# Value slots of a fused two-block transformer kernel: each product of 512 columns written as two of 256

## The chip, the cores and the metric

The kernel runs on one core of one Trainium2 chip. The metric is the device time of the core in microseconds, less being better. Before the change the median of three runs is 1130.42 us (1130.38 to 1130.47).

## What is computed

The input is one sequence of 256 tokens of width 1024 in float32. Two hybrid layers (an mLSTM branch, a gated linear attention branch and a sparse attention branch side by side) are followed by a block of feed-forward, mixer and feed-forward. Almost all of the arithmetic is a product with a large weight matrix. For this change the products matter whose result is wanted with tokens on the partitions, that is the "value" columns:

```python
p = split_columns(rmsnorm(x, norm_g) @ w_in)      # ml_v, gla_v, dsa_v, dsa_q, dsa_k among its columns
...
z = n @ w_in[l]
v = z[..., 2 * A_WIDTH:3 * A_WIDTH]
zg = jax.nn.gelu(z[..., 3 * A_WIDTH:])
```

## The kernel before, in words

All weights are one long list of 364 "slots". A slot is 128 partitions by 1024 float32, and one transfer of 512 KB (line 301) brings it to `raw`. ScalarE (line 480) rounds it into part 0 of `ring`, the high part in the format fp32r. GpSimd (line 366, twice 512 columns) or, for some slots, VectorE (line 1000) writes the difference as part 1, the low part. `raw` and `ring` hold five slots each. The activations `xs` are kept as a high and a low part too. A product with a weight slot is three TensorE passes (`PARTS`): weight high by x high, weight low by x high, weight high by x low.

TensorE takes the slots in order. Each slot begins with a wait for its low part (`arrived`, `here`) and its last product signals `slots_used`, which lets ScalarE round a later slot into its place. Three forms of slot exist:

- `tile_product` (line 1713): the weight tile is stationary, `xs` of 256 tokens is the moving operand; 24 products of 256 columns for a slot.
- `sum_slot` (line 1798): the same with `ys` moving; 24 products of 256 columns.
- `value_slot` (line 1776): here a tile of 128 tokens of `xs` is stationary and 512 columns of the weights in `ring` are moving; for each of two token tiles, two k tiles and three passes there is one product of 512 columns, 12 for a slot. Four such slots in a row complete two PSUM banks, one for each token tile. With `by_tile` the 512 columns lie in four runs of 128.

There are 56 value slots: in each of the two hybrid layers the slots 6 to 13, 18 to 25 and 42 to 49 (table `VALUE_SLOTS`), and in the mixer the slots 8 to 15. Between slots TensorE does small work of the attention branches, "jobs" (tables `jobs` and `jobs2`), for instance `level` (line 1958), `index_logits` (1907, 1909), `ml_scores` (2032, 2035), `scores2` (2201, 2202). Of the 56 value slots 20 follow another slot directly (6, 7, 10, 12, 18, 42, 43, 44 of each layer, and 8, 10, 11, 12 of the mixer), and 36 follow a job. Each of the 672 products has a weight load (LDWEIGHTS) of its own.

Of the kernel before, what the change touches and what calls it, by code (L numbers as in the profile page):

```python
# [28 lines left out]
P = 128  # L29
D = 1024  # L30
T = 256
# [123 lines left out]
def build(nc, d, out):  # L155
    ctx = ExitStack()
    with ctx:
        def sb(name, shape, dt=F32):
            return ctx.enter_context(nc.sbuf_tensor(name, shape, dt))
# [15 lines left out]
        xs = sb("xs", [P, KT, 2, T], F32R)  # L175
# [53 lines left out]
        def branch(k, part):  # L229

            return ys[:, k, part, :] if k < 4 else xs[:, k - 4, part, :]
# [18 lines left out]
        ps = [ctx.enter_context(nc.psum_tensor(f"ps{b}", [P, 512], F32)) for b in range(8)]  # L250
# [1439 lines left out]
        def _(pe):  # L1690
            mm = pe.matmul
# [13 lines left out]
            def tile_product(bank, half, slot, rhs, ks=range(KT), at=0, ready=None, freed=False, first=True, final=True):  # L1705

                order = [(k, w, x) for k in ks for w, x in PARTS]
                if ready:
                    order = [(k, w, 0) for k in ks for w in (0, 1)] + [(k, 0, 1) for k in ks]
                for i, (k, wp, xp) in enumerate(order):  # L1710
                    if ready and wp == 0:
                        ready(k, xp)
                    last = mm(ps[bank][:, half * T:(half + 1) * T],  # L1713
                              ring[:, slot % RING, wp, (at + k) * P:(at + k + 1) * P], rhs(k, xp),
                              start=(first and i == 0), stop=(final and i == len(order) - 1))
                    if freed and (wp, xp) == PARTS[-1] and k < KT - 1:
                        last.then_inc(S["xs_free"], 1)
                return last
# [49 lines left out]
            def value_slot(banks, slot, q, by_tile=False):  # L1768

                for tt in range(2):  # L1770
                    for k in range(2):
                        for j, (wp, xp) in enumerate(PARTS):
                            w = ring[:, slot % RING, wp, k * 512:(k + 1) * 512].rearrange("p (j c) -> p j c", j=4)
                            if by_tile:
                                w = ring[:, slot % RING, wp, :].rearrange("p (j k c) -> p k j c", j=4, k=2)[:, k]
                            last = mm(ps[banks[tt]][:, :].rearrange("p (j c) -> p j c", j=4),  # L1776
                                      xs[:, 2 * q + k, xp, tt * P:(tt + 1) * P], w,
                                      start=(q == 0 and k == 0 and j == 0), stop=(q == 3 and k == 1 and j == 2))
                last.then_inc(S["slots_used"], 1)

            def sum_slot_lo_last(slot, at, y_lo):
# [60 lines left out]
            for it in range(LAYERS):  # L1842
# [238 lines left out]
                for p in range(IN_SLOTS):  # L2081
                    done = results_at(p)
                    if p in VALUE_SLOTS:
                        r, q = VALUE_SLOTS[p]
# [7 lines left out]
                        if r == EARLY:  # L2092
                            pe.wait_ge(S["x_hi"], it * KT + 2 * q + 2)
                            pe.wait_ge(S["x_lo"], it * KT + 2 * q + 2)
                        value_slot((r % 4, (r + 1) % 4), p, q, r < R_GQ)
                    else:
                        r = done[0]
# [158 lines left out]
            for p in range(MIX_IN_SLOTS + GATE_SLOTS):  # L2256
                slot = MIX_AT + p
                if 8 <= p < 16:
                    r, q = 8 + (p - 8) // 4 * 2, p % 4
                    if q == 0:  # L2260
                        m_bank_free(r)
                        m_bank_free(r + 1)
                    here(slot)
                    if r == M_EARLY:
                        pe.wait_ge(S["x_hi"], LAYERS * KT + 2 * q + 2)
                        pe.wait_ge(S["x_lo"], LAYERS * KT + 2 * q + 2)
                    value_slot((r % 4, r % 4 + 1), slot, q)
                else:
                    r = m_results_at(p)[0]
                    if r == 2:  # L2270
                        here(slot)
                        around_squares(2, slot, 3)
                    elif r > 1:
                        m_bank_free(r)
                        here(slot)
                        tile_product(r % 4, 0, slot, xs_part,
                                     freed=(r == M_EARLY - 1 or r == 31)).then_inc(S["slots_used"], 1)
                    if r == 1:
                        here(MIX_AT)
                        here(MIX_AT + 1)  # L2280
                        first_two((0, MIX_AT), (1, MIX_AT + 1), xs_part, early_ready(3))
                for job, *which in jobs2.get(p, ()):
                    job(*which)
            for n in range(KT):
# [7 lines left out]
                for g in range(2):  # L2292
                    last = tile_product(n % 4, g, slot, lambda k, part: branch(4 * g + k, part), range(4), at=4 * g,
                                        ready=(lambda k, part: pe.wait_ge(
                                            S["b_lo" if part else "b_hi"], 4 * g + k + 1)) if n == 0 else None)
# [28 lines left out]
            for b in (5, 6):  # L2324
                for c in range(2):
                    last = mm(ps[b][:, c * P:(c + 1) * P], rms[:, 512 + c:513 + c].broadcast_to((P, P)), ident,
                              start=True, stop=True)
# [129 lines left out]
```

## Time and profile before

| | |
|---|---|
| median of three runs | 1130.42 us |
| the profiled execution's own time | 1130.05 us |
| its span, first to last instruction | 1128.3 us |
| TensorE (PE) busy | 1118.7 us, 8976 products |
| TensorE weight loads (PEld) busy | 1065.4 us, 8976 loads |
| VectorE, ScalarE, GpSimd busy | 711.0, 663.6, 732.1 us |
| granted TensorE clock | 0.998 |

Products overlap in the records: one of 256 columns is recorded as 276 ns long though the next starts 113 ns later. So the time that a product costs is read from stretches of equal products in the chain of waits (its time divided by its count), not from the recorded length of one.

### The profile page before, as it was taken

What the parts mean: (1) busy time and instruction counts of PE and PEld (TensorE: products, weight loads), DVE (VectorE), ACT (ScalarE), POOL (GpSimd) and SP (SyncE); (2) the same over time, 40 slices, a digit from 0 to 9 for tenths busy, and PEclk for the clock granted to TensorE, in tenths of its full rate; (3) what the DMA queues carried; (4) which work ended last, traced back from release to release, by engine and by line L of the source; (5) the groups of instructions that cost most, each with busy time, mean ns of one, the idle gap of its engine ahead of it and who ended that gap; (6) DMA issues with size and microseconds to landing.
All of it is one profiled execution on the core that took longest, in us unless ns stands there. A gap on an engine that the chain in (4) does not pass through costs nothing.

```text
span 1128.3 us, 22357 instructions
## 1 busy us (share of the span) xinstructions
PE 1118.7 (99%) x8976; PEld 1065.4 (94%) x8976; DVE 711.0 (63%) x1262; ACT 663.6 (59%) x1096; POOL 732.1 (65%) x577
## 2 busy tenths in 40 slices
PE   8999999999999999999999999999999999999997
PEld 7888998999988799899999999999899999999997
DVE  6886644566588775264857655556768667655554
ACT  7676854476577577446646544446566547544444
POOL 6787697667488868865765654445865774544442
PEclk9999999999999999999999999999999999999999
DMA  8553354546555534545566755664644654665650
GB/s 319 185 180 130 121 181 151 171 160 211 169 169 169 167 123 150 187 135 186 169 206 202 234 189 190 197 200 144 221 146 138 200 187 163 225 196 190 188 186 38
DMA packets 63895, 199.49 MB, mean 177 GB/s; under 512 B 6992, under 2 KB 17968, under 8 KB 63792
## 3 DMA queue, kind: packets, MB, share of 16 engines
q1 hardware_dynamic: 61920, 194.99, 52.9%
q10 hardware_dynamic: 1872, 3.08, 0.8%
q8 instruction: 71, 1.16, 0.4%
q14 instruction: 32, 0.26, 0.1%
HBM read 196.21 MB, written 1.84 MB: 176 GB/s over the span
## 4 chain that ended last, share of the span: by engine, by line
PE 97%; ACT 1%; DMA 1%; DVE 0%; issue 0%; POOLq 0%; SPq 0%; ACTq 0%
PE ps L1713 51%; PE ps L1798 19%; PE ps L1776 14%; PE ps L1958 2%; PE ps L1749 1%; PE ps L2052 1%; PE ps L2135 1%; PE ps L2032 1%; PE ps L2062 1%; DMA x<-in_x 1%; PE ps L1732 1%; PE ps L1993 1%; PE ps L2053 0%; PE ps L1932 0%; PE ps L2019 0%; PE ps L2035 0%
## 5 line engine op out<-in xcount | busy, mean ns | idle before, releaser
L366 POOL TENSOR_TENSOR ring<-raw,ring 128x512 fp32r<-128x512 f32 x516 | 699.6, 1362 | 370.6 <-ACT ring L480 349.4
L1713 PE MATMUL ps<-xs,ring 128*128 128x256 f32 x5040 | 598.5, 278 | 1.0 <-DVE mq L1038 0.9
L1713 PEld LDWEIGHTS ps<-xs,ring 128*128 128x128 f32 x5040 | 582.9, 188 | 5.9 <-issue 3.2
L480 ACT ACTIVATE ring<-raw 128x1024 fp32r<-128x1024 f32 x364 | 383.2, 1057 | 215.4 <-PE ps L1713 119.2
L1798 PE MATMUL ps<-ys,ring 128*128 128x256 f32 x1920 | 224.4, 276 | 0.0
L1798 PEld LDWEIGHTS ps<-ys,ring 128*128 128x128 f32 x1920 | 220.7, 188 | 0.0
L1000 DVE TENSOR_TENSOR ring<-raw,ring 128x1024 fp32r<-128x1024 f32 x106 | 141.7, 1337 | 68.4 <-ACT ring L480 67.8
L1776 PE MATMUL ps<-ring,xs 128*128 128x512 f32 x672 | 165.0, 398 | 0.0
L1776 PEld LDWEIGHTS ps<-ring,xs 128*128 128x128 f32 x672 | 123.6, 188 | 26.8 <-issue 1.3
L1313 DVE SCALAR_TENSOR_TENSOR ca<-ps,par,ca 128x253 f32<-128x253 f32 (+2 forms) x96 | 45.9, 478 | 34.4 <-ACT ca L564 33.0
L1457 DVE SCALAR_TENSOR_TENSOR ca<-ps,rms 128x256 f32<-128x256 f32 x44 | 18.6, 422 | 48.6 <-PE ps L1713 48.6
L1452 DVE SCALAR_TENSOR_TENSOR ex<-ps,rms 128x256 f32<-128x256 f32 x44 | 18.6, 423 | 45.1 <-PE ps L1713 44.9
L1062 DVE TENSOR_TENSOR ys<-y,ys 128x256 fp32r<-128x256 f32 x32 | 31.7, 991 | 19.5 <-ACT ys L721 19.5
L809 ACT ACTIVATE ys<-ca 128x256 fp32r<-128x256 f32 x44 | 18.4, 418 | 34.8 <-DVE ca L1466 34.8
L1062 DVE TENSOR_TENSOR ys<-ca,ys 128x256 fp32r<-128x256 f32 x44 | 30.4, 691 | 11.0 <-ACT ys L809 11.0
L581 ACT ACTIVATE ex<-ps 128x256 f32<-128x256 f32 x32 | 12.2, 382 | 35.0 <-PE ps L1713 34.9
L1462 DVE TENSOR_TENSOR ca<-ca,ex 128x256 f32<-128x256 f32 x44 | 30.8, 700 | 1.5
L564 ACT ACTIVATE ca<-ps,par 128x256 f32<-128x256 f32 x32 | 17.9, 560 | 21.0 <-PE ps L1713 21.0
L497 ACT ACTIVATE xs<-x,par 128x256 fp32r<-128x256 f32 x40 | 16.7, 496 | 12.8 <-DVE x L1072 9.6
L1369 DVE SCALAR_TENSOR_TENSOR ps<-ex,ps 128x256 f32<-128x256 f32 x32 | 13.6, 424 | 15.2 <-ACT ex L581 15.2
L1466 DVE SCALAR_TENSOR_TENSOR ca<-ex,ca 128x256 f32<-128x256 f32 x44 | 22.2, 505 | 1.4
L1749 PE MATMUL ps<-xs,ring 128*128 128x256 f32 x192 | 22.4, 276 | 0.0
(288 smaller groups left out, 1033.0 us busy)
## 6 DMA issues: line engine op xcount, KB each, us to landing
raw<-in_w SPq DMA_DIRECT2D x364, 512.0 KB, 3.5
y<-bias_rows SPq DMA_DIRECT2D x6, 256.0 KB, 4.6
out_y<-y SPq DMA_DIRECT2D x4, 256.0 KB, 2.3
const<-in_const SPq DMA_DIRECT2D x1, 896.0 KB, 12.3
bias_rows<-lg ACTq DMA_DIRECT2D x1, 768.0 KB, 7.1
x<-in_x ACTq DMA_DIRECT2D x1, 512.0 KB, 4.4
x<-in_x SPq DMA_DIRECT2D x1, 512.0 KB, 6.7
dec<-in_wT ACTq DMA_DIRECT2D x1, 512.0 KB, 3.6
```

The lines of the kernel that those rows point to most:

```text
L366: last = pool.tensor_tensor(ring[:, g % RING, 1, part], raw[:, g % RAW, part], ring[:, g % RING, 0, part].bitcast(F32), ALU.subtract)
L480: act.activation(ring[:, g % RING, 0, :], raw[:, g % RAW, :], ACT.Copy).then_inc(S["hi"], 1)
L1000: tt(ring[:, g % RING, 1, :], raw[:, g % RAW, :], ring[:, g % RING, 0, :].bitcast(F32), ALU.subtract).then_inc(lo[g % RAW], 1)
L1062: tt(ys[:, at, 1, :], src, ys[:, at, 0, :].bitcast(F32), ALU.subtract).then_inc(S["y_lo"], 1)
L1313: ins = stt(dst[:, late:T], bank[:, 0:T - late], w[:, j:j + 1], dst[:, late:T], ALU.mult, ALU.add)
L1462: step(tt(ca[:, f % 2, :], ca[:, f % 2, :], ex[:, 2 + f % 2, :], ALU.mult))
L1466: stt(ca[:, f % 2, :], ex[:, f % 2, :], 1.0, ca[:, f % 2, :], ALU.add, ALU.mult)\
L1713: last = mm(ps[bank][:, half * T:(half + 1) * T], ring[:, slot % RING, wp, (at + k) * P:(at + k + 1) * P], rhs(k, xp), start=(first and i ...
L1749: return mm(ps[bank][:, 0:T], ring[:, slot % RING, wp, k * P:(k + 1) * P], rhs(k, xp), start=start, stop=stop)
L1776: last = mm(ps[banks[tt]][:, :].rearrange("p (j c) -> p j c", j=4), xs[:, 2 * q + k, xp, tt * P:(tt + 1) * P], w, start=(q == 0 and k == 0 ...
L1798: ins = mm(ps[4 + n // 2][:, n % 2 * T:(n % 2 + 1) * T], ring[:, slot % RING, wp, n * P:(n + 1) * P], ys[:, at, xp, :], start=(first and n ...
L1958: last = mm(second(ps[6 + e][:, (2 * tt + pr) * P:(2 * tt + pr + 1) * P]), kk[rows, keys], second(qq[rows, queries]), start=True, stop=True)
```

## The change

In `value_slot` each product of 512 columns becomes two of 256, one for each half of the bank, with the same stationary tile of `xs`. The bank is started by the first of them alone; the second half relies on the cleared state of the bank. Nothing else is changed: the order of slots and jobs, the waits and the signals stay.

```diff
-                            last = mm(ps[banks[tt]][:, :].rearrange("p (j c) -> p j c", j=4),
-                                      xs[:, 2 * q + k, xp, tt * P:(tt + 1) * P], w,
-                                      start=(q == 0 and k == 0 and j == 0), stop=(q == 3 and k == 1 and j == 2))
+                            for hf in range(2):
+                                last = mm(ps[banks[tt]][:, hf * T:(hf + 1) * T].rearrange("p (j c) -> p j c", j=2),
+                                          xs[:, 2 * q + k, xp, tt * P:(tt + 1) * P], w[:, 2 * hf:2 * hf + 2],
+                                          start=(q == 0 and k == 0 and j == 0 and hf == 0),
+                                          stop=(q == 3 and k == 1 and j == 2), skip_group_check=True)
                 last.then_inc(S["slots_used"], 1)
```

## Rows read from the trace of the kernel before

**Rows 1.** The page: busy time of the engines, and the granted clock.

```profile
PE 1118.7 (99%) x8976; PEld 1065.4 (94%) x8976; DVE 711.0 (63%) x1262; ACT 663.6 (59%) x1096; POOL 732.1 (65%) x577
...
PEclk9999999999999999999999999999999999999999
```

**Rows 2.** The page: the chain that ended last, shares by line.

```profile
PE ps L1713 51%; PE ps L1798 19%; PE ps L1776 14%; PE ps L1958 2%; PE ps L1749 1%; PE ps L2052 1%; PE ps L2135 1%; PE ps L2032 1%; PE ps L2062 1%; DMA x<-in_x 1%; PE ps L1732 1%; PE ps L1993 1%; PE ps L2053 0%; PE ps L1932 0%; PE ps L2019 0%; PE ps L2035 0%
```

**Rows 3.** Groups of instructions: busy us, mean ns of one, idle before, releaser.

```profile
L1713 PE MATMUL ps<-xs,ring 128*128 128x256 f32 x5040 | 598.5, 278 | 1.0 <-DVE mq L1038 0.9
L1713 PEld LDWEIGHTS ps<-xs,ring 128*128 128x128 f32 x5040 | 582.9, 188 | 5.9 <-issue 3.2
...
L1776 PE MATMUL ps<-ring,xs 128*128 128x512 f32 x672 | 165.0, 398 | 0.0
L1776 PEld LDWEIGHTS ps<-ring,xs 128*128 128x128 f32 x672 | 123.6, 188 | 26.8 <-issue 1.3
```

**Rows 4.** The waits: who waited for whom, us in total, times, longest.

```profile
POOL ring L366 <- ACT ring L480: 349.4, 145, 9.5
ACT ring L480 <- PE ps L1713: 119.2, 81, 2.0
...
ACT ring L480 <- PE ps L1776: 22.7, 12, 3.0
```

**Rows 5.** The chain in order of time (start, us, what): slots that follow slots.

```profile
138.85 19.05 PE ps L1713 x168
157.91 8.24 PE ps L1776 x36
...
203.92 29.94 PE ps L1713 x264
...
261.84 43.52 PE ps L1798 x384
```

**Rows 6.** The chain, 185 to 194.5 us: slots of both forms around a job.

```profile
185.00 2.75 PE ps L1776 x12
187.75 0.86 PE ps L2032 x4
188.61 0.45 PE ps L2035 x4
189.06 5.47 PE ps L1713 x48
```

**Rows 7.** The chain, 66 to 111 us: slots before and after line 1958.

```profile
81.70 2.96 PE ps L1776 x12
84.66 1.04 PE ps L1958 x16
...
107.40 2.94 PE ps L1713 x24
```

**Rows 8.** The chain in the mixer, 805 to 835 us.

```profile
805.97 11.01 PE ps L1776 x48
...
817.52 0.43 PE ps L2202 x2
817.96 2.75 PE ps L1776 x12
...
828.51 2.74 PE ps L1713 x24
...
831.80 0.43 PE ps L2202 x2
832.23 2.83 PE ps L1713 x24
```

**Rows 9.** The chain: slots 4 to 7 of the first layer, 6 and 7 of the second.

```profile
23.42 5.92 PE ps L1713 x48
29.34 5.60 PE ps L1776 x24
...
322.56 5.49 PE ps L1776 x24
```

## Prediction

> **What bounds the kernel now.** I began with the busy times and the clock [rows 1]. TensorE is busy for 1118.7 of 1128.3 us, and its clock is granted in full in every slice, so it runs at the upper of its two levels, 2.4 GHz, throughout. The shares of the chain say the same [rows 2]: lines 1713, 1798 and 1776, all products with weights, are 84% of it, and the value slots (1776) are 14% or about 158 us. The groups [rows 3] show no idle time ahead of the 672 products of line 1776. The suppliers are not late either: GpSimd, which finishes a slot, stands 349.4 us waiting for ScalarE, and ScalarE stands 119.2 us waiting for line 1713 and 22.7 us for line 1776 to free a place [rows 4]. So the end is set by how fast TensorE takes products one behind the other, and each nanosecond saved or lost on one of them reaches the end, unless the supply becomes late; it would have to be late by a few tens of nanoseconds for each slot, where it now waits for TensorE.
>
> **The prices.** The question is then whether two products of 256 columns take longer than one of 512. The chain in order of time answers it for this kernel. Where slots follow slots [rows 5], 36 products of 512 columns take 8.24 us, 228.9 ns each. The 168 products of 256 columns ahead of them take 19.05 us, 113.4 ns each; 264 later ones take 29.94 us (113.4 ns) and 384 of line 1798 43.52 us (113.3 ns). A slot is thus 2.747 us in the old form and 24 x 113.4 = 2.722 us in the new one: the change would gain 0.025 us for such a slot.
>
> Behind a job [rows 6] the old form takes 2.75 us for a slot, and two slots of line 1713 behind a similar job 5.47 us, 2.735 us each: 0.015 us better. Around line 1958 [rows 7] a value slot takes 2.96 us, a slot of line 1713 entered from the same line 2.94 us. I take 0.01 us for all slots behind jobs, since both numbers are rounded to it and other slots of line 1713 show 2.74 us [rows 8].
>
> There is an exception. Some slots of line 1713 run at a slower pace throughout, not only at their start: behind line 2202 a slot takes 2.83 us [rows 8], 118 ns a product, while the value slot that stands behind the same line takes 2.75 us, 229 ns a product of 512. Three more slots of that pair of lines later on repeat it. The slow pace is also carried from slot to slot: in the first layer the value slots 6 and 7 take 5.60 us, 233.3 ns a product, behind 48 products of line 1713 that take 5.92 us, while the same two slots in the second layer take 5.49 us, 228.8 ns [rows 9]. So a product has two paces here, 113.4 or 118 ns for 256 columns and 229 or 233 ns for 512. In the slow pace two halves cost 236 ns against 233, and, worse, a place that is quick for 512 columns may be slow for 256, as behind line 2202: 2.83 - 2.75 = 0.08 us lost for a slot.
>
> **The change part by part.**
> - Removed: 672 products of 512 columns with their loads. Added: 1344 of 256 with 1344 loads. Loads take 188 ns each [rows 3], longer than the pace of 113 ns, but line 1713 has a load for each product too, and keeps the pace; so I cost the added loads at nothing. That cover is gone only if a load could no longer start early; the whole 188 ns would then be seen.
> - Value slots that follow slots, without the mixer's 10 to 12 and the first layer's 6 and 7: 15 x 0.025 = 0.38 us gained.
> - Value slots behind jobs, without the mixer's 9, 13 and 15, which stand behind line 2202: 33 x 0.01 = 0.33 us gained.
> - The mixer's slots 9, 13 and 15, and 10 to 12 that follow 9 directly and would inherit its pace: 6 x 0.08 = 0.48 us lost.
> - The first layer's 6 and 7: 2 x 2.83 against 5.60 us, 0.06 us lost.
> - Nothing is moved past a wait or a queue, and the last product of a slot ends where it did: signals, evacuations and transfers follow within tens of nanoseconds. The start flag stands on one product in place of one; nothing waits on it.
>
> The sum is -0.38 - 0.33 + 0.48 + 0.06 = -0.17 us. On the profiled execution's 1130.05 us (span 1128.3) this is 1129.9 us; the median of the runs is 0.37 us above it, so I give 1130.42 - 0.17, rounded to 1130.2 us. No row shows a 256-column product with `ring` moving and `xs` stationary, so the pace is bounded from both sides: below by 113.3 ns in every slot, 672 x (228.9 - 226.6) = 1.5 us gained; above by 118 ns in every slot, 56 x 0.08 = 4.5 us lost. I take the quick pace except where a slot of line 1713 shows the slow one, because nearly all of its rows are quick.
>
> A rule speaks against the change. If 512 columns took 228.9 ns because of a cost for each product, two products would pay it twice. The rows say that there is none: doubling the 256 columns of line 1713 gives 226.8 ns, less than 228.9. By the Trainium skill (TensorE: Matmul & The Clock Gate, "Back-to-back issue gap") products at the full clock start N / 2.4 + 2.5 ns apart, and so one more product costs 2.5 ns: an estimate of 672 x 2.5 = 1.7 us lost. The trace disagrees with both figures of that rule, 113.4 ns where it gives 109.2 and 228.9 where it gives 215.8.
>
> **The rivals.** A measurement of this kernel can tell about 0.2%, 2.3 us, from no change; I judge them by that.
>
> 1. *Quick pace everywhere.* The slow pace comes from something at line 2202 that fits line 1713 only. Then 20 x 0.025 + 36 x 0.01 to 0.015 gives 0.9 to 1.0 us, up to 1.5 us by the pace alone: 1128.9 to 1129.5 us. For it: most rows are quick. Against: value slots do fall into the slow pace [rows 9].
> 2. *A surcharge for each product with these operands.* The 2.1 ns by which 512 columns exceed twice 113.4 may belong to the moving operand in `ring` and be paid once a product. Then a pair takes 226.8 + 2 x 2.1 = 231.0 ns, and 672 x 2.1 = 1.4 us are lost: 1131.8 us. For it: the surplus is seen only where `ring` is moving. Against: it could as well grow with the columns. The skill's rule named above points the same way.
> 3. *The slow pace everywhere (slower).* The place is the entry into a value slot behind a job; the slow pace, once entered, lasts to the next job, as in [rows 9]. Each slot loses 0.08 us, all 56 lose 4.5 us: 1134.9 us. It decides from 35 slow slots on (35 x 0.08 less 21 x 0.025 is 2.3 us). For it: line 2202 does just this. Against: behind lines 2035 and 1958 line 1713 is quick [rows 6, 7], and these jobs stand ahead of most value slots.
> 4. *Halves quicker than any row of that form.* Four products behind one another at line 2035 take 0.45 us, 112.5 ns each [rows 6]. At that pace a pair takes 225 ns and 672 x 3.9 = 2.6 us are gained: 1127.8 us. Nothing but that small job speaks for it.
> 5. *The loads are seen.* If the second load of the same tile of `xs` couldn't start under the first half, 672 x up to 188 ns = 126 us would be lost, 1256.7 us. Against: the first two passes of a k tile share their tile already, and the group is not slower for it than 228.9 ns.
>
> That the change doesn't do what it says (the two products or their loads being merged again) is ruled out by the counts: the first two passes share a stationary tile now, and there are still 672 loads for 672 products [rows 3]. If it were so, nothing would change.
>
> **How the numbers follow.** The forecast (a mixture of paces, 1129.6 to 1131.0) has a chance of 0.45, the quick pace everywhere 0.25, the surcharge 0.14, the slow pace everywhere or nearly so 0.09, quicker halves 0.05, seen loads 0.02. The first three are all within 0.2%: 0.84. Faster by more has 0.05, slower by more 0.11. The range is to hold the first three cases, the lower bound of rival 1 and the estimate by the rule included: 1128.6 to 1132.3 us.
>
> **What the profile of the changed kernel would show.** There should be 9648 products and as many loads, with 1344 of 256 columns in the value line; in the chain, stretches of 24 of them at 2.72 to 2.75 us where 12 stood at 2.75 us, and 2.83 us in the mixer behind line 2202 (now a few lines lower). The waits of ScalarE and GpSimd should be unchanged to a few us, the clock full. The prediction is wrong if the value slots' share of the chain changes by over 2.3 us, if idle time shows ahead of them, or if time changes outside of them.

## Result: slower by 0.25%, and the profile after

The changed kernel takes 1133.21 us (median of nine runs, 1132.11 to 1133.72) against 1130.42 us; the ratio is 1.0025 with a 95% interval of 1.0016 to 1.0033. That is 2.8 us slower, outside the range of 1128.6 to 1132.3 us and against a chance of 0.11 for slower by more than 0.2%. The profiled execution of the changed kernel has a span of 1131.0 us, 2.7 us longer than before, so its trace holds about the loss of the medians. (The own times of the two profiled executions lie 3.4 us apart, 1133.46 and 1130.05 us; 0.7 us of that lies outside the spans.)

The page of the kernel after, busy times and clock; they answer to [rows 1]:

```profile
PE 1121.3 (99%) x9648; PEld 1098.9 (97%) x9648; DVE 710.5 (63%) x1262; ACT 663.6 (59%) x1096; POOL 731.5 (65%) x577
...
PEclk9999999999999999999999999999999999999999
```

The groups of the same page, which answer to [rows 3]:

```profile
L1713 PE MATMUL ps<-xs,ring 128*128 128x256 f32 x5040 | 598.8, 278 | 1.2 <-DVE mq L1038 1.1
...
L1777 PE MATMUL ps<-ring,xs 128*128 128x256 f32 x1344 | 167.4, 281 | 0.0
L1777 PEld LDWEIGHTS ps<-ring,xs 128*128 128x128 f32 x1344 | 160.3, 188 | 2.3 <-issue 1.3
```

The counts are as forecast, the clock is full, line 1713 is what it was (598.8 us against 598.5), and no idle time stands ahead of the value line. Its busy time went from 165.0 to 167.4 us. So the loss is in the pace of the half-products, and the chain in order of time (start, us, what) shows where. First, value slots that follow slots and enter behind line 1713, against [rows 5]:

```profile
139.68 19.05 PE ps L1713 x168
158.73 8.16 PE ps L1777 x72
```

Three slots in 8.16 us, 113.3 ns a half-product; they took 8.24 us. This is the small gain that the forecast counted. Next, value slots behind jobs, and a pair of slots of line 1713, against [rows 6]:

```profile
181.26 2.83 PE ps L1777 x24
...
186.05 2.83 PE ps L1777 x24
...
190.19 5.47 PE ps L1713 x48
```

The first and the last of these stretches stand right behind the same job, `ml_scores`. Line 1713 still takes 2.735 us a slot there, but the value slots now take 2.83 us where they took 2.75, 118 ns a half-product. The level job and the mixer, against [rows 7, 8]:

```profile
73.68 3.02 PE ps L1777 x24
```

```profile
808.06 11.31 PE ps L1777 x96
...
820.36 2.82 PE ps L1777 x24
...
823.83 2.83 PE ps L1777 x24
```

Of the 56 value slots 42 end at a pace of 118 ns a half-product and 14 at 113.4 ns. The difference of each slot can be summed from the starts of the products in the two traces. Of the 42, most lose 0.06 to 0.08 us (three, slots 6 and 7 of the first layer and 13 of the second, which were in the slow pace before too, lose 0.03 us), together 2.87 us. The 14 gain 0.02 to 0.04 us each, together 0.38 us. That is 2.5 us net of the 2.7 us between the spans; of the rest, line 1713 is 0.35 us longer in the same count and smaller lines make up the remainder in both directions. Twelve of the 14 quick slots follow a slot or a stream of line 1713 directly; the other two (8 of the first layer, 9 of the second) stand behind a job and come back to the quick pace. All such counts are of one traced execution each.

### The profile page after: what moved, and what is told of

Its sections match the earlier page's. It is cut to its first block, busy times and chain, and to the rows that moved or that the text cites. A ratio compares the mean times of both kernels' runs of the same rounds, so it can differ in the third digit from the quotient of the medians.

```text
span 1131.0 us, 23701 instructions
## 1 busy us (share of the span) xinstructions
PE 1121.3 (99%) x9648; PEld 1098.9 (97%) x9648; DVE 710.5 (63%) x1262; ACT 663.6 (59%) x1096; POOL 731.5 (65%) x577
## 4 chain that ended last, share of the span: by engine, by line
PE 96%; DMA 1%; ACT 1%; DVE 1%; SPq 0%; issue 0%; POOLq 0%; ACTq 0%
PE ps L1713 51%; PE ps L1800 19%; PE ps L1777 14%; PE ps L1960 2%; PE ps L1749 1%; DMA par<-in_par 1%; PE ps L2054 1%; PE ps L2137 1%; PE ps L2034 1%; PE ps L2064 1%; PE ps L1995 1%; PE ps L2055 0%; PE ps L1934 0%; PE ps L2021 0%; PE ps L2037 0%; PE ps L2204 0%
## 5 line engine op out<-in xcount | busy, mean ns | idle before, releaser
L1713 PE MATMUL ps<-xs,ring 128*128 128x256 f32 x5040 | 598.8, 278 | 1.2 <-DVE mq L1038 1.1
L1777 PE MATMUL ps<-ring,xs 128*128 128x256 f32 x1344 | 167.4, 281 | 0.0
L1777 PEld LDWEIGHTS ps<-ring,xs 128*128 128x128 f32 x1344 | 160.3, 188 | 2.3 <-issue 1.3
```

The costliest lines, as they stand in the source:

```text
L1713: last = mm(ps[bank][:, half * T:(half + 1) * T], ring[:, slot % RING, wp, (at + k) * P:(at + k + 1) * P], rhs(k, xp), start=(first and i ...
L1777: last = mm(ps[banks[tt]][:, hf * T:(hf + 1) * T].rearrange("p (j c) -> p j c", j=2), xs[:, 2 * q + k, xp, tt * P:(tt + 1) * P], w[:, 2 * ...
```

## The experiments

They ran beside the kernel before on the same chip; its median is given each time. Theories are named by the letters of the expectations: A is that the slow pace is picked up at the entry behind a job and kept, B that any half-product costs more.

**Which slots lose.** `value_slot` gets a flag that is true for slots which follow another slot directly.

The diff is against the kernel before, in part:

```diff
-                            last = mm(ps[banks[tt]][:, :].rearrange("p (j c) -> p j c", j=4),
...
+                            step = 2 if follows else 4
+                            for c in range(0, 4, step):
+                                last = mm(ps[banks[tt]][:, c * P:(c + step) * P].rearrange("p (j c) -> p j c", j=step),
...
```

> Only the 20 value slots that follow another slot directly are split; the 36 behind jobs keep products of 512 columns. Theory A (the pace of 118 ns is picked up at the entry behind a job and kept by half-products): slots that follow a quick slot run at 2.72 us, so the kernel gains up to 20 x 0.025 = 0.5 us over the kernel before, 1129.9 to 1130.4 us, unless the mixer's slots 10 to 12 (behind slot 9, itself behind a job) are slow, which costs 3 x 0.08 us. Theory B (a surcharge of halves of this kind wherever they stand): 672 x 20/56 = 240 products cost 20/56 of the loss, +1.0 us, 1131.4 us.

Measured: 1130.27 us against 1130.28 (ratio 1.0001, 0.9992 to 1.001). The complement (`not follows`):

> Only the 36 value slots behind jobs are split. Theory A: nearly all of the loss is here, 33 to 36 slots at 2.83 us (3.02 around the level job) in place of 2.75 (2.96), +2.5 to +3.0 us against the kernel before, 1132.9 to 1133.4 us. Theory B: 36/56 of the loss, +1.8 us, 1132.2 us.

Measured: 1132.61 us against 1130.28 (1.0021, 1.0012 to 1.003). The loss is mainly in the slots behind jobs, as A says: by their traces the value slots of e1 take 0.3 us more than before and those of e2 2.1 us. By the medians alone B's 1.0 and 1.8 us aren't excluded; what speaks against B are the quick stretches, 8.16 us for three split slots in the changed kernel. But in e1 the chain of the mixer holds something that A did not foresee:

```profile
805.67 11.22 PE ps L1778 x84
```

These are one whole slot of 12 products and three split ones of 24. A whole slot took 2.75 us at this place before (11.01 us for four, [rows 8]); that leaves 8.47 us for the split ones behind it, 118 ns a half-product, though the slot ahead of them was at the quick 229 ns. So halves can be slow behind a whole slot that was quick.

**A whole first product.** The narrow form of A was tried the other way round: the first product of each slot stays whole. The rest of the edit is that of e1.

```diff
...
+                            step = 2 if tt or k or j else 4
...
```

> All slots are split, except that the first product of each slot keeps its 512 columns. If the pace is set by how the second product's load falls behind the first product at the entry (theory A in its narrow form: behind a job the gap from first to second start is about 203 ns with 256 columns and 314 ns with 512), a whole first product lets the later ones start quickly: slots at 2.72 to 2.75 us, -0.5 to -1 us, about 1129.7 us. If the slow pace is a property of halves of this kind (theories B and C), 11/12 of the loss stays, +2.5 us, 1132.9 us.

Measured: 1134.26 us against 1130.28 (1.0036, 1.0024 to 1.0049), worse than with all products split, and against the narrow form. Even the three slots behind the quick stream of line 1713 are slow now:

```profile
158.50 8.48 PE ps L1778 x69
```

They took 8.16 us with all products split and 8.24 us with none. Less the three whole products at 229 ns this is 118 ns for each of the 66 halves. Of the 56 slots 50 are slow now, against 42. It isn't a strict rule: slots 13, 20 and 24 of both layers, all behind jobs, run their halves at 113.4 ns though each begins with a whole product.

**The order of the products.** The half was made the outer loop (e3, which keeps `PARTS`), then the passes were also reordered so that no tile of x is loaded twice in a row (e5, whose diff against the changed kernel this is, in part):

```diff
                 for tt in range(2):
-                    for k in range(2):
-                        for j, (wp, xp) in enumerate(PARTS):
...
-                            for hf in range(2):
+                    for hf in range(2):
+                        for k in range(2):
+                            for j, (wp, xp) in enumerate(((0, 0), (0, 1), (1, 0))):
...
```

> All 56 slots are split, but for each token tile the six products of the left half come first, then the six of the right half, so the PSUM half changes once and the stationary tile is not loaded twice for each pass. Theory A as it stands (entry alone, the order of products does not matter): 118 ns in some 42 slots as in the changed kernel, +2.8 us, 1133.2 us. Theory C (the slow pace is held by the repeated load of the same tile and the alternation between halves, which line 1713 does not have): the pace falls back to 113.4 ns as in line 1713, 56 slots gain, -0.9 to -1.5 us, 1129 to 1129.5 us.

> All slots split, left half outermost, and the three passes in the order high by high, weight high by x low, weight low by x high, so that no two products in a row load the same tile of x; the moving tile is what repeats, as in line 1713. Theory D (the slow pace is kept because a stationary tile is loaded twice in a row, which line 1713 never does): slots behind jobs fall back to 113.4 ns within a few products, 56 quick slots, -0.9 to -1.5 us against the kernel before, about 1129.2 us. Theory E (the pace once picked up is kept by any slot with x stationary and the ring moving, whatever the order): 118 ns in some 42 slots again, +2.6 us, 1132.9 us.

Measured: 1132.93 us against 1130.28 (1.0026, 1.0017 to 1.0035) and 1133.00 us against 1130.44 (1.0024, 1.0014 to 1.0033). Behind the same `ml_scores` a slot of e5 still takes 2.83 us:

```profile
167.42 2.83 PE ps L1777 x24
```

In both kernels 39 slots are slow. Only slots of the first layer differ from the changed kernel: 6, 7, 9 and 10 are quick here and 8 is slow. Theories C and D are refuted: neither the change of PSUM halves after each product nor a repeated load is the cause. The same order of passes in `tile_product` (line 1713) and in whole value products:

> The kernel before, value slots whole, but line 1713 takes its passes as high by high, weight high by x low, weight low by x high, so that each weight tile is loaded twice in a row. Theory D: line 1713 slots behind jobs, about 50 of them, keep the pace of 118 ns (2.83 us in place of 2.74), up to +4 us, and slots that follow one another carry it, perhaps more. Theory E: no change beyond 0.5 us, 1130.3 us.

> The kernel before, whole products of 512 columns, with the order of passes high by high, weight high by x low, weight low by x high. In the kernel before the start-to-start time is 226 ns behind the first pass, whose tile the next product loads again, and 229 to 231 ns behind the other two. Theory D extended to whole products: with no tile repeated the 226 ns goes or moves, up to 672/3 x 4 ns = +0.9 us. Theory E: the pace of 228.9 ns stays, within 0.3 us of the kernel before, 1130.3 us.

Measured: 1130.42 us against 1130.44 (1.0, 0.9991 to 1.0009) and 1130.55 us against 1130.44 (1.0001, 0.9992 to 1.0009). Nothing moves, which agrees.

**The loads.** Three of four value slots use stationary tiles of 64 tokens; the results of the other 64 are left out.

```diff
+                            n = 64 if q else P
                             for hf in range(2):
-                                last = mm(ps[banks[tt]][:, hf * T:(hf + 1) * T].rearrange("p (j c) -> p j c", j=2),
-                                          xs[:, 2 * q + k, xp, tt * P:(tt + 1) * P], w[:, 2 * hf:2 * hf + 2],
+                                last = mm(ps[banks[tt]][0:n, hf * T:(hf + 1) * T].rearrange("p (j c) -> p j c", j=2),
+                                          xs[:, 2 * q + k, xp, tt * P:tt * P + n], w[:, 2 * hf:2 * hf + 2],
```

> The changed kernel, with stationary tiles of 64 tokens in place of 128 in three of four value slots (all but the first slot of each group of four): the results of the other 64 tokens of each tile are left out there. The 42 slots so changed have loads of half the columns. Theory F (the pace of halves is set by the weight load, which barely fits under 256 columns): those slots run at or below 113.3 ns even behind jobs, -1 us or more against the kernel before. Theory G (the columns of the product set it, the load only its start): 118 ns stays behind jobs, +2.7 us, as in the changed kernel.

Measured: 1132.15 us against 1130.44 (1.0016, 1.0007 to 1.0025). One line of the trace gives the loads (min, median, max ns), and the chain the slots behind a job:

```profile
L1778 PEld LDWEIGHTS ps<-ring,xs x1344: 132/134/192, 28.7 to 828.4; 128*64 128x64 f32 x144, 128*128 128x128 f32 x48
```

```profile
77.66 2.80 PE ps L1778 x24
...
86.06 2.83 PE ps L1778 x24
```

The first slot has loads of 64 columns (134 ns in place of 188), the other is a first slot of its group with loads of 128. Halving the load takes 0.03 us from a slot (116.7 in place of 118 ns a half-product), but it doesn't come back to 113.4 ns. So the pace is not that of a load that barely fits, though the load has a part in it.

**Whose operands.** Only the operands of the 1344 half-products were changed, so these kernels compute something else than the reference and serve for their time alone. The diff is that of e11, which exchanges both; e9 has its stationary tile alone, e10 its moving operand alone.

```diff
-                                          xs[:, 2 * q + k, xp, tt * P:(tt + 1) * P], w[:, 2 * hf:2 * hf + 2],
+                                          ring[:, slot % RING, wp, (2 * k + tt) * P:(2 * k + tt + 1) * P], xs[:, 2 * q + k, xp, :].rearrange("p (j c) -> p j c", j=2),
```

> The changed kernel with the stationary tile taken from the ring (the same slot) in place of xs, the moving operand unchanged; the values computed are not the reference's, only the number and shape of products and loads are kept. Theory H (loads from xs keep the slow pace): behind jobs the pace falls to 113.4 ns within some products as in line 1713, -0.9 to -1.5 us against the kernel before. Theory I (a moving operand in the ring keeps it): 118 ns in some 42 slots, +2.7 us.

> The changed kernel with the moving operand taken from xs (256 tokens) in place of the ring, the stationary tile from xs as now; the values are again not the reference's. Theory H: 118 ns stays in some 42 slots, +2.7 us against the kernel before. Theory I: quick behind most jobs, -0.9 to -1.5 us. If both this and e9 are slow, it is neither operand alone but their place in the program; if both are quick, it is the pair.

> A control: in the value slots, 24 products with the stationary tile from the ring and the moving operand from xs, the operands of line 1713, at the same places behind the same jobs and with the same PSUM halves; the values are not the reference's. If the operands decide (H or I): quick behind most jobs, about 113.4 ns, -0.9 to -1.5 us. If the place in the program or the alternation of PSUM halves decides: 118 ns in some 42 slots, +2.7 us.

Measured: e9 1137.22 us (1.0061, 1.0048 to 1.0075), e10 1137.81 us (1.0066, 1.0052 to 1.008), e11 1130.56 us (1.0004, 0.9994 to 1.0013), all against 1130.24. The chain of e9, then of e11, at the three slots behind line 1713 and at a slot behind a job:

```profile
159.14 8.62 PE ps L1777 x72
...
169.06 2.87 PE ps L1777 x24
```

```profile
158.04 8.16 PE ps L1777 x72
...
167.51 2.75 PE ps L1777 x24
```

With both operands in one tensor, whichever, all 56 slots run at 119.7 to 120 ns, however they are entered. With the operands of line 1713, at the same places and into the same PSUM halves, only 16 slots are slow and 40 quick. So neither H nor I is right, and e11 rules out that the place in the program makes e9 and e10 slow; it is the pair that counts. But e11 is no faster than the kernel before either.

**Only the quick entries.** The 13 slots 6, 7, 18, 42, 43, 44 of each layer and 8 of the mixer are split.

> Only 13 value slots are split, those entered from a stream of line 1713 or from another such slot: 6, 7, 18, 42, 43, 44 of each layer and 8 of the mixer. By the pace kept from the entry each should take 2.72 us in place of 2.75: at most 13 x 0.025 = 0.3 us gained, 1130.1 us, less 0.1 us if the first layer's two slots enter slowly. That is below what the runs can tell; the chain should show it. If the split has a cost wherever it stands, +0.6 us.

Measured: 1129.94 us against 1130.24 (0.9998, 0.9989 to 1.0006), which can't be told from no change. The chain shows the expected 2.72 us for the mixer's slot:

```profile
800.96 2.72 PE ps L1778 x24
```

**Distance, place or remainder.** In e13 the moving operand is always tile 0 of `xs`, so that the two operands are up to 14 KB apart. In e14 and e15 one line is moved, `xs = sb("xs", [P, KT, 2, T], F32R)`, ahead of `raw` and behind `y`.

> As e10 (both operands from xs), but the moving operand is always tile 0 of xs, so that the two operands lie 0 to 7 tiles (0 to 28 KB... in steps of 2 KB of a partition: 0 to 14 KB) apart, growing from the first to the fourth slot of each group; the values are not the reference's. Theory J (the clash is one of nearness: both operands in the same stretch of memory): the first slot of each group stays at 120 ns, the later ones fall to 118 or 113 ns. Theory K (distance does not matter, the pace depends on something else of the pair): 120 ns in all 56 slots, +7.4 us.

> The changed kernel with xs allocated as the first tensor, ahead of raw and ring; every tensor up to xs moves by 16 KB of a partition, nothing else changes. Theory L (the operands' addresses set the pace): the count of slow value slots, 42 of 56, changes much, and that of line 1713 too; if all were quick, 1129.3 us. Theory M (the roles set it: a load from activations under a stream of weights): again about 42 slow, 1133 us.

> The changed kernel with xs allocated last, behind y. Theory L: the count of slow value slots changes, in this run or in e14 or in both. Theory M: about 42 slow, 1133 us.

Measured: e13 1137.70 us (two runs; 1.0064, 1.0044 to 1.0084), e14 1169.23 us (1.0343, 1.0326 to 1.0361), e15 1163.82 us (1.0294, 1.0279 to 1.031), against 1130.52. Distance, up to 14 KB within the tensor, changes nothing: all 56 slots stay at 120 ns. But the place of one tensor costs 36 us. The chain of e14:

```profile
142.21 20.16 PE ps L1713 x168
162.37 8.64 PE ps L1777 x72
...
270.97 43.54 PE ps L1800 x384
```

Line 1713, which reads `xs` too, went from 113.4 to 120 ns a product, while line 1800, which reads `ys`, is where it was. Summed over the traces of e14 and the changed kernel, line 1713 is 29.4 us longer, the value slots 4.1 us and line 1749 1.2 us, of 36.5 us in all. The addresses in the compiled programs (bytes within a partition) suggest why. In the kernels before and after `ring` starts at 36992 and `xs` at 97856; their remainders modulo 128 are 0 and 64, and every tile within them starts at a multiple of 512 bytes from there. In e14 they start at 53376 and 16512, in e15 `xs` at 211456: the remainders agree. `ys` differs from `ring` by 64 in all of them. In e9, e10 and e13 both operands are in one tensor and agree as well. The pace of e15 is a little better than that of e14, though:

```profile
141.74 19.94 PE ps L1713 x168
161.68 8.54 PE ps L1777 x72
```

That is 118.7 and 118.6 ns a product. Modulo 256 the two kernels differ: `xs` and `ring` agree in e14 and are 128 apart in e15. So the remainder modulo 128 may not be all that counts; no run was made to separate this from the distance, which is larger in e15.

The test is to change 64 bytes of e14 (the diff is against e14; `gap` is never read or written):

```diff
         xs = sb("xs", [P, KT, 2, T], F32R)
+        sb("gap", [P, 16])
         raw = sb("raw", [P, RAW, SLOT])
```

> e14 (xs first in memory) with an unused tensor of 64 bytes behind xs, so that xs and ring again differ by 64 modulo 128. Theory N (the remainder of the two addresses modulo 128 bytes sets the pace): line 1713 is back at 113 ns, the time falls from 1169 us to about 1133 us, with some 42 slow value slots. Theory O (the region or the distance): 1169 us stays.

Measured: 1132.94 us against 1130.37 (1.0024, 1.0013 to 1.0034), 36 us less than e14 and no different from the changed kernel, with the same 42 slow value slots. `xs` has the same address in e14 and e16, and `ring` the same in the kernel before and in e15, yet one of each pair has line 1713 slow; so the difference of the two counts and not the place of either. Its chain:

```profile
139.50 19.05 PE ps L1714 x168
158.55 8.16 PE ps L1778 x72
```

Two other remainders, by a `gap` of 8 and of 24 floats ahead of `xs`:

> The changed kernel with an unused tensor of 32 bytes ahead of xs: xs and ring differ by 96 modulo 128, what follows xs moves along. If 64 is the best remainder and any other clashes partly: line 1713 between 113.4 and 120 ns, 1134 to 1169 us. If 64 is not special but only 0 is bad: 1133 us or, when the slow pace of 118 ns is ended too, 1129.3 us.

> The changed kernel with 96 bytes ahead of xs: xs and ring differ by 32 modulo 128. The same alternatives as for the remainder 96; the two tell whether the sign matters, as it might for loads under streams and the reverse (line 1713 against the value slots).

Measured: e17 1168.16 us (1.0334, 1.0319 to 1.035), e18 1159.89 us (1.0262, 1.0247 to 1.0277), against 1130.37. The chain of e17, then of e18:

```profile
140.99 19.89 PE ps L1714 x168
160.88 8.40 PE ps L1778 x72
...
267.98 45.44 PE ps L1801 x384
```

```profile
140.74 19.61 PE ps L1714 x168
160.34 8.52 PE ps L1778 x72
...
267.11 45.23 PE ps L1801 x384
```

Here `ys` moved along, and its line slowed too, to 118 ns. The sign of the difference matters as well, which the expectation of e18 asked. Stationary minus moving address, modulo 128, is 96 for the value slots of e17 and for line 1713 of e18, and both take 116.7 ns in these stretches; it is 32 for line 1713 of e17 and the value slots of e18, and both take 118.3 to 118.4 ns. (The line of `ys` in e18 fits less well: 117.8 ns where 96 would give 116.7.) Of the four differences tried (0, 32, 64, 96) only 64 gives 113.4 ns, and none brings the value halves behind jobs to it. None of the versions that compute the reference is faster than the kernel before; e12, e1, e6 and e8 can't be told from it.

## Why the prediction was wrong

- *TensorE bounds the kernel and nanoseconds of its pace reach the end*: right. The value slots lose 2.5 us net, and the span is 2.7 us longer. The sign of being wrong that the prediction set, a change of over 2.3 us in the value slots, came.
- *Slots that follow slots, 15 x 0.025 = 0.38 us gained*: they gained 0.07 us. The term is right where the stream ahead is quick (8.16 against 8.24 us for three), in the second layer's slots 6 and 7 too. Slots 10 and 12 of the layers inherited in three of four cases the slow pace of the slot ahead, which I had foreseen for the mixer alone.
- *The mixer's slots at 2.83 us, the first layer's two at 5.66*: right. The six slots of the mixer lost 0.45 us (0.48 forecast; 11.31 us for slots 9 to 12 against 11.01 before), the two of the first layer 0.06 us as forecast.
- *The value slots behind jobs, 33 x 0.01 us gained*: this step failed. In place of 0.33 us gained these slots lost 2.05 us: 31 of them lose 0.03 to 0.08 us each, and only two gain. I took their price from line 1713 behind the same jobs, a product of the same shape with its operands exchanged. e11 shows that this exchange is most of the error: with the operands of line 1713 the same 33 slots lose 0.28 us in the trace, 40 of all 56 are quick and the time is 1130.56 us. It is not all of it, since even then they don't gain. What the step missed is that after a disturbance line 1713 mostly comes back to the quick pace within the slot, and halves with `xs` stationary and `ring` moving did so in 2 of 36 slots behind jobs.
- *Of the rivals*, the third, the slow pace everywhere, is what happened, with 42 slots in place of 56; it decides from 35 on, as worked out, and for 42 its prices give 42 x 0.08 less 14 x 0.025, 3.0 us. It had a chance of 0.09 since I read line 1713's recovery as evidence for the value slots. The second, a surcharge for each product, is refuted by the 8.16 us. The rule of the Trainium skill (TensorE: Matmul & The Clock Gate, "Back-to-back issue gap"), which the page states as the gap of an isolated product, gave an estimate of 1.7 us lost. The trace doesn't bear it out as the cause, since three slots that would have paid it gained 0.08 us; that its sign was right is chance. The added loads being seen (the fifth) did not occur, but they have a part: shorter loads take 0.03 us from a slow slot (e7).
- *Whole products ahead of halves* weren't considered at all; e1 and e4 show that they mostly cost the quick pace.

Shown are: the loss by slots (trace, e1, e2), that the order of products and PSUM halves are not its cause (e3, e5), that which tensor is stationary and which is moving decides how many slots are slow (e11 against the changed kernel), and that 64 bytes between the addresses of the two operands are worth 36 us (e14 against e16). That the remainder modulo 128 bytes is the whole of that rule is not shown (e15). Why halves stay slow behind jobs even 64 bytes apart, and with it the last cause of the loss, is open. One candidate is untested: in all kernels with the pace of 113.4 ns `xs` lies 192 above `ring` modulo 256, so exchanging the roles also turns the difference around, and a distance of 64 modulo 256 was never tried.

## What to carry to other kernels

A price read from products of the same shape is good only for the same operands in the same roles; ask also whether the pace after a disturbance recovers, since a slot of 24 products may keep a state that it entered with. Where TensorE bounds a kernel and its products of 256 columns are each preceded by a load, look at the pace in the chain (here 113 or 117 to 120 ns) and at the addresses of the two operands before any reordering. In e14 64 bytes of padding gave back 36 us, 13 times what the change under study cost. The kernel before had the good difference without anyone having chosen it, so a tensor added or resized between the two can undo it without anyone touching a product.

## What the runs showed of the hardware that I had not expected

- Products of 256 columns, each with its load, start 113.3 ns apart at best where the addresses of stationary and moving tile differ by 64 modulo 128 bytes (before, after, e16), and 120 ns where they agree modulo 256 (e9, e10, e13, e14); e15, where they agree modulo 128 only, has 118.7 ns in its stretch of 168. Where the stationary address is 96 above the moving one it is 116.7 ns, where it is 32 above 118.4 ns (19.61 us for 168 in e18, 19.89 in e17).
- At a difference of 64 a second steady pace of 118 ns exists. It lasts for whole slots, is mostly carried from slot to slot, and is entered behind jobs (34 of 36 value slots) and behind products of 512 columns (50 of 56 slots in e4).
- Loads of 64 columns take 134 ns in the records against 188 ns for 128.
